# A decoder trunk with eight routed experts: the experts run in the order second, first, third and on

## What is computed

```python
logits = xf @ router_w                       # 256 tokens x 8 experts
top_val, top_idx = lax.top_k(logits, 2)
gates = softmax(top_val)
# for every expert e, for the tokens that chose it:
ys = (silu(x @ w_gate[e]) * (x @ w_up[e])) @ w_down[e]     # 1024 -> 2816 -> 1024
out[token] += gate[token, e] * ys
```

## Time and profile before

| | us |
|---|---|
| median of 3 runs (lowest to highest) | 1466.91 (1465.32 to 1468.29) |
| the profiled execution, its own time | 1468.1 |
| its span in the trace | 1466.3 |
| PE busy | 1414.9 (96%) |
| DVE, ACT, POOL busy | 505.3, 407.2, 107.5 |
| read from HBM | 383.77 MB |
| experts, from the first product of expert 0 to the last of expert 7 | 699.4 to 1450.4 |

### The profile page before, as it was taken

One profiled execution on the slowest core, in us unless ns is written; L12 is line 12 of the kernel. 1 busy time (PEld: TensorE's weight loads), 2 busy tenths in 40 slices (PEclk: granted clock), 3 DMA queues, 4 the chain that ended last, 5 costly groups with the idle time before them and its releaser, 6 DMA issues.

```text
span 1466.3 us, 23253 instructions
## 1 busy us (share of the span) xinstructions
PE 1414.9 (96%) x10140; PEld 1021.0 (70%) x10140; DVE 505.3 (34%) x747; ACT 407.2 (28%) x707; POOL 107.5 (7%) x133
## 2 busy tenths in 40 slices
PE   7999999999999999998999999999998999999996
PEld 7979988888888979988555645555544455555553
DVE  5667546666665657545100010101010100011112
ACT  5467436434345467444100000000000000000001
POOL 6200000000006000000100000101010100010100
PEclk9999999999999999998999999999999999999998
DMA  9308533555552217526746679999999996489995
GB/s 362 112 3 324 190 116 115 186 187 192 194 200 91 84 72 287 188 101 258 288 176 276 274 293 421 421 420 420 421 421 421 421 421 270 175 342 373 421 421 207
DMA packets 55138, 387.32 MB, mean 264 GB/s; under 512 B 6368, under 2 KB 6752, under 8 KB 9216
## 3 DMA queue, kind: packets, MB, share of 16 engines
q1 hardware_dynamic: 54112, 384.07, 66.1%
q10 hardware_dynamic: 432, 1.08, 0.2%
q0 software_dynamic: 496, 0.74, 0.2%
HBM read 383.77 MB, written 2.10 MB: 263 GB/s over the span
## 4 chain that ended last, share of the span: by engine, by line
PE 85%; DMA 6%; DVE 4%; ACT 3%; issue 1%; SPq 0%; DVEq 0%; ACTq 0%
PE banks L1845 40%; PE banks L1601 9%; PE banks L1603 9%; PE banks L1602 9%; PE banks L1774 6%; DMA raw_of_parts<-in_pieces_dram 4%; PE banks L1776 3%; DMA raw<-in_pieces_dram 2%; PE banks L1824 2%; PE banks L1809 2%; PE banks L1895 1%; PE banks L1721 1%; PE banks L1749 1%; PE banks L1625 1%; ACT w_high L827 1%
## 5 line engine op out<-in xcount | busy, mean ns | idle before, releaser
L1180 DVE TENSOR_TENSOR w_low<-raw,w_high 128x2048 fp32r<-128x2048 f32 x93 | 214.8, 2311 | 134.0 <-ACT w_high L827 133.9
L827 ACT ACTIVATE w_high<-raw 128x2048 fp32r<-128x2048 f32 x93 | 178.0, 1915 | 68.5 <-PE banks L1776 65.5
L1845 PE MATMUL banks<-raw,token_rows 128*64 128x256 f32 (+3 forms) x1480 | 161.3, 352 | 3.1 <-DMA raw<-in_pieces_dram 3.0
L1845 PE MATMUL banks<-raw_of_parts,token_rows 128*32 128x128 f32 (+4 forms) x1448 | 154.7, 344 | 2.8 <-DMA raw_of_parts<-in_pieces_dram 2.8
L1845 PEld LDWEIGHTS banks<-raw,token_rows 128*64 128x64 f32 (+2 forms) x1480 | 93.8, 132 | 71.6 <-issue 48.0
L1601 PE MATMUL banks<-rows,w_high 128*128 128x256 f32 x480 | 137.4, 286 | 2.0 <-DVE rows L1181 2.0
L1845 PEld LDWEIGHTS banks<-raw_of_parts,token_rows 128*64 128x64 f32 (+2 forms) x1448 | 94.5, 132 | 63.2 <-issue 42.5
L1601 PE MATMUL banks<-w_high,rows 128*128 128x256 f32 x480 | 137.4, 286 | 0.0
L1602 PE MATMUL banks<-rows,w_high 128*128 128x256 f32 x480 | 136.6, 285 | 0.0
L1603 PE MATMUL banks<-rows,w_low 128*128 128x256 f32 x480 | 136.6, 285 | 0.0
L1603 PE MATMUL banks<-w_high,rows 128*128 128x256 f32 x480 | 135.8, 283 | 0.0
(11 more groups left out here) (220 smaller groups left out, 1836.7 us busy)
## 6 DMA issues: line engine op xcount, KB each, us to landing
raw<-in_pieces_dram SPq DMA_DIRECT2D x183, 1024.0 KB, 7.2
raw_of_parts<-in_pieces_dram SPq DMA_DIRECT2D x90, 1024.0 KB, 17.8
raw_more<-in_pieces_dram SPq DMA_DIRECT2D x56, 1024.0 KB, 17.6
raw_of_mixed<-in_pieces_dram SPq DMA_DIRECT2D x28, 1024.0 KB, 19.2
phase<-in_mem_dram SPq DMA_DIRECT2D x2, 1024.0 KB, 6.7
early<-in_constants_dram SPq DMA_DIRECT2D x1, 1088.0 KB, 14.4
h_res<-in_x_dram SPq DMA_DIRECT2D x2, 512.0 KB, 4.2
phase<-in_mix_norm_post_dram SPq DMA_DIRECT2D x2, 512.0 KB, 4.4
```

Source lines behind the costliest of these rows:

```text
L827: return act.activation(out_, in_, ACT.Copy, scale=scale)
L1180: return dve.tensor_tensor(out_, in_, plain(high), ALU.subtract)
L1845: return pe.matmul(dst, stay, move, start=start, stop=stop, skip_group_check=True)
```

## The change

A table `EXPERT_AT` maps the place in the sequence to the expert: place 0 holds expert 1, place 1 holds expert 0, the others are as before. Weights are laid out in DRAM by place, the counts, ranks and gates are read by `EXPERT_AT[e]`, and `STRAIGHT` has the class-3 code at places 1 and 5 in place of 0 and 5. No instruction is added on an engine's straight line beyond what the class brings.

```diff
+EXPERT_AT = (1, 0, 2, 3, 4, 5, 6, 7)
...
-STRAIGHT = {0: 3, 5: 3}
+STRAIGHT = {EXPERT_AT.index(0): 3, EXPERT_AT.index(5): 3}
...
                 for kind, name in (("gate", "moe_w_gate"), ("up", "moe_w_up")):
-                    put(piece(e, kind, s, i), given[name][0, e][rows, at])
+                    put(piece(e, kind, s, i), given[name][0, EXPERT_AT[e]][rows, at])
                 first = s * WIDE + i * FFC
-                put(piece(e, "down", s, i), given["moe_w_down"][0, e][first:first + FFC])
+                put(piece(e, "down", s, i), given["moe_w_down"][0, EXPERT_AT[e]][first:first + FFC])
...
-            return eng.value_load(count_i[0:1, e:e + 1], min_val=0, max_val=SEQ)
+            return eng.value_load(count_i[0:1, EXPERT_AT[e]:EXPERT_AT[e] + 1], min_val=0, max_val=SEQ)
...
             def places(e):
                 pool.wait_ge(gathered, ROW_PAIRS * e)
-                for t in range(TT):
-                    pool.tensor_scalar(place[:, t, :], iota, rank[:, t, e:e + 1], chosen[:, t, e:e + 1],
+                n = EXPERT_AT[e]
+                for t in range(TT):
+                    pool.tensor_scalar(place[:, t, :], iota, rank[:, t, n:n + 1], chosen[:, t, n:n + 1],
```

More of the change, by code:

```diff
@@ L795, in gated_places @@
                 pool.wait_ge(spread_full, e)
+                n = EXPERT_AT[e]
                 for t in range(TT):
-                    g = gate[:, t, e:e + 1]
+                    g = gate[:, t, n:n + 1]
                     for slots in (slice(0, HALF_BLOCK), slice(P, SEQ)):
-                        pool.tensor_scalar(place_g[:, t, slots], iota[:, slots], rank[:, t, e:e + 1], g, ALU.is_equal, ALU.mult)
-                    ins = pool.tensor_scalar(place_g[:, t, HALF_BLOCK:P], iota[:, HALF_BLOCK:P], rank_twice[:, t, e:e + 1], g,
+                        pool.tensor_scalar(place_g[:, t, slots], iota[:, slots], rank[:, t, n:n + 1], g, ALU.is_equal, ALU.mult)
+                    ins = pool.tensor_scalar(place_g[:, t, HALF_BLOCK:P], iota[:, HALF_BLOCK:P], rank_twice[:, t, n:n + 1], g,
                                              ALU.is_equal, ALU.mult)
@@ L1366, in find_places @@
             def find_places(e):
+                n = EXPERT_AT[e]
                 for t in range(TT):
-                    dve.tensor_scalar(place[:, t, :], iota, rank[:, t, e:e + 1], chosen[:, t, e:e + 1],
+                    dve.tensor_scalar(place[:, t, :], iota, rank[:, t, n:n + 1], chosen[:, t, n:n + 1],
                                       ALU.is_equal, ALU.mult).then_inc(place_ready, 1)
```

## The result

The changed kernel takes 1452.8 us, the median of four runs (1450.55 to 1455.33), against 1466.33 us for four runs of before: a ratio of 0.9907 with a 95% interval of 0.9886 to 0.9927. A second series, with five runs of the changed kernel, gave 1454.79 us and a ratio of 0.9922 (0.9908 to 0.9935) to the before runs of that series (median 1465.91). The gain is thus 11 to 13.5 us. The forecast had 1454.6 us in a range of 1452.0 to 1458.5.

A forecast was written before the change was run, and what follows sets the result against it. The prediction took PE's work plus class-1 experts starved by the weight stream as the bound; one expert going from 81.99 to 69.74 us saves 12.3 us, from a median of 1466.91 to 1454.6 us, range 1452.0 to 1458.5.

The forecast's parts named there:

- The term of the sum: Experts' part: one class-1 expert goes from the stream's pace, 81.99 us, to PE's, 69.74, saving 12.3 us.
- the other price given, 224.4: Places 0 and 1 together: 224.4 us by separate prices; the forecast took 224.7, with the share carried whole.
- A reading of the windows: Second half cut by expert: expert 0 takes 147.6 us, class-1 experts 70 to 85, expert 5 151.2.
- Pieces are there in place 0: Place 0, the first expert: weight pieces land before they are due, so no wait and a cost of 65.9 us.
- number 32 ... 9 us to spare, the least of all: Last weight piece of place 0: lands at 754.3, due at 763.3, the tightest piece with 9 us of slack.
- The class-3 expert in place 1 fills the ring: Place 1: takes 158.47 us, needs a piece only every 4.7 us, and the ring is full again before its end.
- Other engines: Gather, silu, DVE and SP work around the first experts stays covered: priced at nothing, or a few us once.
- The pace of the stream: Weight DMA runs at 421 GB/s, 81.99 us an expert; the skill's 358 GB/s would give 96.6 and a 27 us gain.
- No gain, because PE is the bound: Whole kernel: PE, busy 96%, is the bound, so about 1466.9 us; chance 0.04 for under 0.2% by either road.
- The front that starves: Place 0: stream restart over 9 us late eats the gain, at worst 1466.9 us; no gain by either road 0.04.
- The larger gain: Third class-1 expert of the run loses its waits too, 4.9 us more, giving 1449.7 us; chance 0.03.
- The clock: Place 0: PE's clock falls back to half, 65.9 us of work takes twice as long, giving 1520.5 us; chance 0.03.

The follow-up runs named there:

- e3: Changed kernel, with SP also waiting ahead of piece 14 until PE has used piece 9, so the front restarts late: 1461.44 us.
- e6: Changed kernel, with SP issuing the residual's stores behind piece 7 in place of piece 13: 1453.91 us.
- e8: Changed kernel with expert 7 in place 0 and expert 1 last, order 7 0 2 3 4 5 6 1: 1453.14 us.
- e9: Kernel of before with expert 1 moved behind expert 5, order 0 2 3 4 5 1 6 7: 1462.16 us.
- e10: Changed kernel run again, unaltered, beside the one before, for the spread: 1454.79 us.
- e4: Both class-3 experts first, then six class-1 experts, order 0 5 1 2 3 4 6 7: 1497.50 us, ratio 1.0217 to the kernel of before.
- e5: Changed kernel with only the table altered, two class-1 experts at the front, order 1 2 0 3 4 5 6 7: 1454.92 us.
- e1: Kernel of before with only half of each later weight piece loaded, PE's instructions unchanged: 1450.64 us, ratio 0.9898 to before.
- e2: Changed kernel with only half of each later weight piece loaded: 1448.40 us, ratio 0.9890 to the kernel of before.
- e7: Changed kernel with order 1 2 0 3 4 5 6 7 and the residual's stores issued early, both together: 1455.19 us.

## Why the prediction was right

**The term of the sum.** The prediction took 12.3 us for one class-1 expert moved from the stream's pace, 81.99 us, to PE's, 69.74. The place at the stream's pace is gone, and none took its stead. Of the 13.5 us in the experts' part, 12.3 are this term. The other 1.2 us: places 0 and 1 took 224.26 us, not 224.7 (the share of one product, carried whole, was 0.4 too much; the other price given, 224.4, was nearer), and the third expert of the run took 73.80 us, not 74.61. That last figure is 73.6 to 74.0 in the profiles after, e3, e6, e8, e9 and e10, and 74.48 in e4. Why it is 74.61 in before is seen beside e9, which has the same order of classes up to there: counted from the start of place 1, SP issues pieces 50 to 102 at the same moments to 0.01 us in both, but pieces 67 to 99, and 131, the last of the third expert, land 0.9 to 1.0 us later in before, behind single late pieces, and 74.61 - 73.60 is that 1.0 us. So the 0.8 us is most likely chance in the landings and no work of the change. The forecast had no term for it, and it flatters the 13.5 us.

**A reading of the windows.** The prediction took the lengths of the experts, 147.6 and 151.2 us among them, from windows whose cuts lie some 7 us ahead of the next expert's first gate product. The lengths are 154.97 and 158.47 us, and the sum used these.

**Pieces are there in place 0.** Right: 65.76 us with no wait (65.9 forecast), and 65.77 in e6 and e8. The slack behind it was off: 9 us forecast, 6.8 to 6.9 measured by e3 and confirmed by e5. The step that failed is "number 32 ... 9 us to spare, the least of all". The first piece of the next place is tighter, and the stream loses 1.7 us behind its restart. It did not touch the sum, as 6.8 is more than nothing, but with two experts at the front it would have: 3.3 us of loss by my 9, 5.3 measured.

**The class-3 expert in place 1 fills the ring.** Right: 158.50 us against 158.47 forecast, at 298 GB/s on average, the stream full at first and idle later, and 73.23 and 69.74 us behind it, as forecast, to the hundredth.

**Other engines.** Right: from the first product to 1430 us, PE waits for nothing but pieces in the profile after. The forecast had 4 to 5 us of waits beside the 11.4 us of before; booked are 2.7 us, and what they cost is 4.1 us of length. The prediction set a length beside booked idle time there.

**The pace of the stream.** 420 to 422 GB/s again wherever PE is starved of pieces; the last expert of e4 has 402 on average, as its window ends behind the last piece. The lower limit of the Trainium skill's page (DMA: Bandwidth & Descriptors) did not show on this core, and the 27 us that it would have given did not come.

**The rivals.** No gain, because PE is the bound: the 96% is the busy share of products, whose ends are modelled, and says nothing of a single stage. PE's work sets the length of seven places in eight, but e1 and e2 show that the order's worth is the stream alone. The front that starves is a real mechanism, as e3 shows, with its threshold 2.1 us nearer than I put it. It did not come here: between the landings of pieces 13 and 14 lie 7.4 us, not the 23 us between SP's issues. The larger gain, 4.9 us for the third expert's waits, did not come in the changed kernel; e2 shows it is there to have (3.9 us) and e5 and e7 that another order pays for it elsewhere. The clock stayed at 1.00 in place 0, and place 0 took 65.7 to 65.8 us in all seven profiles that have a class-1 expert there and the restart at its time or earlier (after, e2, e5, e6, e7, e8, e10); what would make the clock fall was not tried.

**The medians.** 1452.8 and 1454.79 us for the same code stand on both sides of 1454.6. The experts' part repeats within 0.2 us in e6, e8 and e10; in the profiles the rest of the spread is from before the experts.

## What to carry to other kernels

Where a stream of equal pieces feeds stages of unequal length through a ring, compare, stage by stage, the length that the stream needs with the length that the engine needs: the short stages lose their difference only once the lead is used up, and the long ones fill it again and waste what is over. Spread the short stages, so that none runs when the lead is gone, and count the lead ahead of the first stage as one more filling; the price of a starved stage is the stream's length minus its own work, so the lightest stage, often the last, pays most. Check the slack at the first piece of the next stage, not at the last of this one.

## What the runs showed of the hardware

Two profiles of the same code begin their experts at 699.79 and 696.01 us. Ahead of the experts their granted clocks differ in two windows. The changed kernel first, then e10:

```profile
240.00:280.00 40.00, 37.35 (x222) 32.87 (x221) 28.47 (x27) 21.21 (x34) 0.00 (x0) 0.96 0.42 146
440.00:480.00 40.00, 36.82 (x285) 35.27 (x284) 20.41 (x26) 20.75 (x36) 25.90 (x27) 0.91 0.30 108
```

```profile
240.00:280.00 40.00, 37.34 (x228) 32.64 (x227) 28.88 (x28) 21.96 (x36) 0.00 (x0) 1.00 0.43 149
440.00:480.00 40.00, 36.22 (x300) 35.05 (x301) 23.49 (x30) 21.22 (x34) 27.62 (x27) 1.00 0.33 115
```

At 0.96 and 0.91 of full speed for 40 us each, PE spends about 3 us and 7 us of them at the lower level of 1.2 GHz, half of the rate. In finer windows these are the stretches from 251 to 254.5 us, at the first gate products of the dense channel mixer, and from 445 to 452 us. Ahead of both PE had stood still for DVE: for 0.81, 0.56 and 1.27 us ahead of the first, for 2.18 and 0.33 us ahead of the second. The same product inside and behind the first of them:

```profile
253.73 0.63 PE L1778 MATMUL banks<-rows,w_high 128*128 128x512 f32 x1
...
256.14 0.39 PE L1778 MATMUL banks<-rows,w_high 128*128 128x512 f32 x1
```

Set beside e10 instruction by instruction, the first profile is 0.2 us behind ahead of the first stretch, 1.75 us at its end, 1.7 to 2.0 us ahead of the second and 3.7 us behind it, and no more than 0.3 us is gained or lost from there to the first expert. So nearly all of the 3.8 us arises in these two stretches. e10 has the waits for DVE too (2.7 and 3.8 us of idle time in its two windows, against 2.7 and 3.2), and its clock stayed at 1.00 there; why it fell in one execution and not in the other stays open. The four runs of the first series fit: 1455.33, 1453.47, 1452.12 and 1450.55 us at mean clocks of 0.990, 0.991, 0.992 and 0.994. So the spread of 5 us between runs of one kernel goes with the clock, and in the two profiles it is the clock ahead of the experts; no run was made to force it.
